# Two-block transformer, float32 as hi and lo halves: four raw weight slots for five, the relative-bias table moved in parts, the first Silu of an FFN earlier

## The reference

```
for l in range(DEPTH):                                   # block 1, DEPTH = 2
    h = h + 0.5 * swiglu(rms_norm(h, ffn1_norm[l]), w1, w3, w2)
    h = h + token_mixer(rms_norm(h, mix_norm[l]), ...)   # attention + pooling branches
    h = h + 0.5 * swiglu(rms_norm(h, ffn2_norm[l]), w1, w3, w2)
h = rms_norm(h, final_norm)
for l in range(DEPTH):                                   # block 2
    x = x + 0.5 * rmsnorm(swiglu_2(rmsnorm(x, ffn1_pre_g[l]), ...), ffn1_post_g[l])
    ...   # y = sum of 3 gated branches (SSD scan, retention, windowed attention) @ w_out
    x = x + rmsnorm(y, mix_post_g[l])
    x = x + 0.5 * rmsnorm(swiglu_2(rmsnorm(x, ffn2_pre_g[l]), ...), ffn2_post_g[l])

swiglu(u) = (silu(u @ w1) * (u @ w3)) @ w2               # d_ff = 2816
```

## Time and profile before

| | us |
|---|---|
| median of 3 runs (lowest to highest) | 2753.46 (2751.01 to 2755.84) |
| the profiled execution | 2757.64 |
| its span, first to last instruction | 2755.9 |
| TensorE busy in it | 2631.7 (95%) |
| VectorE busy | 1544.3 (56%) |
| ScalarE busy | 1222.1 (44%) |
| DMA queue of the weights, share of 16 engines | 50.1% |
| mean granted clock of TensorE | 0.97 of full |

### The profile page before, as it was taken

The page is one execution under the profiler, slowest core; times in us unless marked ns, Lnnn a source line. Parts: engine busy times, 40 slices in busy tenths (PEclk is TensorE's granted clock), DMA queues, the critical chain, the costliest instruction groups (busy, mean ns, idle before and its releaser), DMA issues.

```text
span 2755.9 us, 30036 instructions
## 1 busy us (share of the span) xinstructions
PE 2631.7 (95%) x12238; PEld 2189.7 (79%) x12238; DVE 1544.3 (56%) x1787; ACT 1222.1 (44%) x1530; POOL 54.1 (2%) x71
## 2 busy tenths in 40 slices
PE   7799999999998999999998998999999998998999
PEld 6688778888887887788877877888888877877887
DVE  5345655454565545545556476545555556485554
ACT  5335444444453444445444353544545444453543
POOL 0000000000000000000000000000000000000000
PEclk9899999999999999999999997999999999998999
DMA  6765355555643555655543341555655542442553
GB/s 226 181 223 169 119 163 192 184 184 184 222 160 113 183 184 183 217 185 192 185 163 103 126 151 61 177 191 176 198 192 199 175 161 91 139 138 75 184 192 122
DMA packets 309753, 459.02 MB, mean 167 GB/s; under 512 B 18112, under 2 KB 207856, under 8 KB 309360
## 3 DMA queue, kind: packets, MB, share of 16 engines
q1 hardware_dynamic: 306976, 452.83, 50.1%
q10 hardware_dynamic: 2640, 4.26, 1.1%
HBM read 452.84 MB, written 4.19 MB: 166 GB/s over the span
## 4 chain that ended last, share of the span: by engine, by line
PE 87%; DVE 5%; ACT 3%; issue 2%; DMA 2%; SPq 0%; DVEq 0%; POOL 0%; ACTq 0%
PE acc L588 46%; PE work L588 32%; PE work L595 2%; PE acc L797 2%; PE work L781 1%; ACT w_hi L1024 1%; DVE w_lo L1337 1%; DMA raw<-ffn_w_dram 1%; DMA raw<-w_ffn_in_dram 1%; PE work L993 1%; DVE field L1528 0%; ACT xt_hi L1070 0%; PE work L623 0%; PE work L810 0%; ACT field L1178 0%
## 5 line engine op out<-in xcount | busy, mean ns | idle before, releaser
L1337 DVE TENSOR_TENSOR w_lo<-raw,w_hi 128x2048 fp32r<-128x2048 f32 (+1 forms) x420 | 953.4, 2272 | 784.9 <-ACT w_hi L1024 784.4
L1024 ACT CAST w_hi<-raw 128x2048 fp32r<-128x2048 f32 (+1 forms) x420 | 795.3, 1895 | 606.5 <-PE acc L588 279.4
L588 PE MATMUL work<-w_hi,xt_hi 128*128 128x512 f32 x1408 | 559.7, 397 | 12.3 <-DVE w_lo L1337 5.4
L588 PE MATMUL work<-w_hi,xt_lo 128*128 128x512 f32 x1408 | 550.4, 391 | 0.0
L588 PE MATMUL work<-w_lo,xt_hi 128*128 128x512 f32 x1408 | 549.7, 390 | 0.0
L588 PE MATMUL acc<-w_hi,yt_hi 128*128 128x512 f32 x1088 | 434.7, 400 | 22.9 <-DVE yt_lo L1348 19.5
L588 PE MATMUL acc<-w_hi,yt_lo 128*128 128x512 f32 x1088 | 430.0, 395 | 0.0
L588 PE MATMUL acc<-w_lo,yt_hi 128*128 128x512 f32 x1088 | 429.9, 395 | 0.0
L588 PE MATMUL acc<-w_hi,xt_hi 128*128 128x512 f32 (+2 forms) x896 | 345.2, 385 | 5.9 <-DVE field L1528 4.3
L588 PE MATMUL acc<-w_lo,xt_hi 128*128 128x512 f32 (+2 forms) x896 | 341.8, 381 | 0.0
L588 PE MATMUL acc<-w_hi,xt_lo 128*128 128x512 f32 (+2 forms) x896 | 341.7, 381 | 0.0
(11 more groups left out here) (162 smaller groups left out, 1732.7 us busy)
## 6 DMA issues: line engine op xcount, KB each, us to landing
raw<-ffn_w_dram SPq DMA_DIRECT2D x264, 512.0 KB, 4.5
raw<-w_in_dram SPq DMA_DIRECT2D x204, 512.0 KB, 4.5
raw<-w_ffn_in_dram SPq DMA_DIRECT2D x176, 512.0 KB, 4.8
raw<-w_ffn_out_dram SPq DMA_DIRECT2D x88, 512.0 KB, 4.3
raw<-w_branch_dram SPq DMA_DIRECT2D x48, 512.0 KB, 4.5
raw<-w_out_dram SPq DMA_DIRECT2D x32, 512.0 KB, 4.4
bias<-b_gate_dram SPq DMA_DIRECT2D x10, 512.0 KB, 7.0
raw<-w_branch_attn_dram SPq DMA_DIRECT2D x8, 512.0 KB, 3.9
```

What stands on the lines that cost most here:

```text
L588: last = nc.tensor.matmul(out, x[:, kt, k], y, start=start and n == 0, stop=stop and n == 2)
L1024: nc.scalar.copy(w_hi[:, slot, 0:n], raw[:, at, 0:n]).then_inc(hi_split[slot], 1)
L1337: nc.vector.tensor_tensor(w_lo[:, at, 0:n], raw[:, at, 0:n], w_hi[:, slot, 0:n].bitcast(F32), ALU.subtract).then_inc(unit_split[slot], 1)
```

## The change

It has four parts. (1) `RAWS` goes from 5 to 4: the load of unit p now waits for unit p-4. (2) ACT stores the table in 8 parts of 384 KB, one each in steps 2 to 8 of the first FFN and the eighth after them, and SP loads it in 4 parts of 512 KB in steps 2 to 5 of the first FFN of block 2; `decay` and `rope2` go from step 0 to step 1. (3) In the entry of an FFN the Silu of row 0 and its `hidden` stand ahead of the square of row 1 and of the cast of unit 3, and those of row 1 ahead of the cast of unit 4. (4) At the passage from block 1 to block 2 the transposes of h come behind the last part of the down product.

```diff
-RAWS = 5
+RAWS = 4
+PIECES = 8
...
-            def second_block():
-
-                sp.wait_ge(h_ready, h_count(number[0, depth - 1, "f2"]))
-                for dst, src in ((decay, a["decay"]), (rope2, a["rope2"])):
-                    sp.dma_start(dst, src).then_inc(blk_loaded, 16)
-                sp.wait_ge(scratch_stored, 16)
-
-                sp.dma_start(rel_bias, bass.AP(a["scratch"].tensor, P - 1,
-                                               [[3 * P - 1, P], [3 * P * P, 16], [1, 2 * P]])) \
-                    .then_inc(blk_loaded, 16)
+            def second_block(j):
+
+                if j == 1:
+                    for dst, src in ((decay, a["decay"]), (rope2, a["rope2"])):
+                        sp.dma_start(dst, src).then_inc(blk_loaded, 16)
+                    sp.wait_ge(scratch_stored, 16 * PIECES)
+                if 2 <= j < 6:
+                    g = j - 2
+                    sp.dma_start(rel_bias[:, 4 * g:4 * g + 4, :],
+                                 bass.AP(a["scratch"].tensor, P - 1 + 4 * g * 3 * P * P,
+                                         [[3 * P - 1, P], [3 * P * P, 4], [1, 2 * P]])) \
+                        .then_inc(blk_loaded, 16)
...
-                early = not block and name == "f1"
-                if early:
+                at = 3 if stage + 1 == len(stages) else 2 if stages[stage + 1][0] > block else block or name == "f2"
+                if at == 0:
                     turn_h(stage + 1, 0)
                 down_part(u + 3 * steps - 1, 1, 0, 2, end=True).then_inc(half_summed, 1)
-                if not early and stage + 1 < len(stages):
+                if at == 1:
                     turn_h(stage + 1, 0)
                 down_part(u + 3 * steps - 1, 1, 1, 2, end=True).then_inc(unit_used[slot], 1)
+                if at == 2:
+                    turn_h(stage + 1, 0)
...
                 turn_hi_rows(stage, 1, range(4))
+                if name != "m":
+                    act.wait_ge(rs_ready, norm_count(block, l, "pre_" + name, 0))
+                    silu(u, 0, 0)
                 square_row(1, 4)
                 split(u + 3)
...
-                for r in range(2):
-                    act.wait_ge(rs_ready, norm_count(block, l, "pre_" + name, r))
-                    silu(0, r)
-                    split(u + 4 + r)
+                act.wait_ge(rs_ready, norm_count(block, l, "pre_" + name, 1))
+                silu(u, 0, 1)
+                split(u + 4)
+                split(u + 5)
...
                         act.wait_ge(table_ready, 2)
-                        act.dma_start(a["scratch"], field[0:16, 5000:5384].unsqueeze(1).broadcast_to([16, P, 3 * P])) \
-                            .then_inc(scratch_stored, 16)
+                    if j >= 2 and stage == 0:
+                        store_table(j - 2)
...
+                def store_table(i):
+
+                    n = P // PIECES
+                    act.dma_start(a["scratch"][:, i * n:(i + 1) * n, :],
+                                  field[0:16, 5000:5384].unsqueeze(1).broadcast_to([16, n, 3 * P])) \
+                        .then_inc(scratch_stored, 16)
...
                 turn_lo_rows(stage, 1, range(4))
+                if name != "m":
+                    dve.wait_ge(rs_ready, norm_count(block, l, "pre_" + name, 0))
+                    hidden(ffn_count(block, l, name, 2 * steps), 0, 0)
                 split(u + 3)
```

More of the change, by code:

```diff
@@ L419, in mixer_small, with ffn @@
                         .then_inc(bias_loaded[i], 16)
-            def ffn(block, name, l, between=lambda: None):
+            def ffn(block, name, l, between=lambda j: None):
                 u = first_unit[block, l, name]
@@ L430, in ffn @@
                         small(block, l, name)
-                        between()
+                    between(j)
                 if name == "f1":
@@ L500, in mixer2, with constants @@
                 chunks("w_out_2", 0, 2)
-            def constants():
+            def constants(j):
+                if j:
+                    return
                 sp.dma_start(field[0:32, 4096:4112], a["rel_bias_2"]).then_inc(consts_loaded, 16)
@@ L510, in constants @@
                     .then_inc(post_loaded, 16)
-            def second_block():
-                sp.wait_ge(h_ready, h_count(number[0, depth - 1, "f2"]))
-                for dst, src in ((decay, a["decay"]), (rope2, a["rope2"])):
-                    sp.dma_start(dst, src).then_inc(blk_loaded, 16)
-                sp.wait_ge(scratch_stored, 16)
-                sp.dma_start(rel_bias, bass.AP(a["scratch"].tensor, P - 1,
-                                               [[3 * P - 1, P], [3 * P * P, 16], [1, 2 * P]])) \
-                    .then_inc(blk_loaded, 16)
+            def second_block(j):
[9 more added lines that the diff above has]
+                        .then_inc(blk_loaded, 16)
             for block in range(2):
                 for l in range(depth):
-                    ffn(block, "f1", l, (second_block if block else constants) if l == 0 else lambda: None)
+                    ffn(block, "f1", l, (second_block if block else constants) if l == 0 else lambda j: None)
                     (mixer2 if block else mixer1)(l)
@@ L1072, in turn_hi_rows, with silu @@
                     last.then_inc(xt_hi_ready, 1)
+            def silu(u, j, r):
+                slot, n = used_count(u + 3 * j if j else u + 1, r)
+                act.wait_ge(unit_used[slot], n)
+                nc.scalar.activation(act_gate[:, r, :], work[2 + r][:, 0:NARROW], ACT.Silu,
+                                     scale=rs[:, r:r + 1]).then_inc(silu_ready, 1)
             def enter(stage, end=None):
@@ L1143, in ffn @@
                         act.wait_ge(table_ready, 2)
-                        act.dma_start(a["scratch"], field[0:16, 5000:5384].unsqueeze(1).broadcast_to([16, P, 3 * P])) \
-                            .then_inc(scratch_stored, 16)
+                    if j >= 2 and stage == 0:
+                        store_table(j - 2)
                     split(u + 6 + 3 * j)
                     for r in range(2):
-                        silu(j + 1, r)
+                        silu(u, j + 1, r)
                     split(u + 7 + 3 * j)
@@ L1151, in ffn @@
                 hidden_halves(steps - 2)
+                if stage == 0:
+                    for i in range(steps - 4, PIECES):
+                        store_table(i)
                 split(n - 1)
-                silu(steps - 1, 0)
+                silu(u, steps - 1, 0)
                 split(n)
-                silu(steps - 1, 1)
+                silu(u, steps - 1, 1)
                 hidden_row(0)
@@ L1205, in mixer1 @@
                 ahead(1)
-                act.wait_ge(scratch_stored, 16)
+                act.wait_ge(scratch_stored, 16 * PIECES)
                 act.wait_ge(rs_ready, norm_count(0, l, "pre_m", 1))
@@ L1414, in norm_final, with hidden @@
                                                    ALU.mult).then_inc(h_ready, 1)
+            def hidden(silus_before, j, r):
+                dve.wait_ge(silu_ready, silus_before + (j * 2 + (r + 1)))
+                nc.vector.scalar_tensor_tensor(hid[:, r, :], work[2 + r][:, NARROW:2 * NARROW], rs[:, r:r + 1],
+                                               act_gate[:, r, :], ALU.mult, ALU.mult).then_inc(hidden_ready, 1)
             def enter(stage, end=None, by=0.5):
@@ L1457, in ffn @@
                 silus_before = ffn_count(block, l, name, 2 * steps)
[L1459 to L1463, removed]
                 def hidden_halves(step):
@@ L1476, in hidden_row @@
                                             yt_hi[:, 2:4, k].bitcast(F32), ALU.subtract).then_inc(hidden_split, 1)
[L1478 to L1481, removed]
+                dve.wait_ge(rs_ready, norm_count(block, l, "pre_" + name, 1))
+                hidden(silus_before, 0, 1)
+                split(u + 4)
+                split(u + 5)
                 for j in range(steps - 2):
@@ L1491, in ffn @@
                     for r in range(2):
-                        hidden(j + 1, r)
+                        hidden(silus_before, j + 1, r)
                     split(u + 7 + 3 * j)
@@ L1496, in ffn @@
                 split(n - 1)
-                hidden(steps - 1, 0)
+                hidden(silus_before, steps - 1, 0)
                 split(n)
-                hidden(steps - 1, 1)
+                hidden(silus_before, steps - 1, 1)
                 hidden_row(0)
@@ L1659, in mixer2 @@
                 ahead(5)
-                dve.wait_ge(blk_loaded, 48 * depth + 48)
+                dve.wait_ge(blk_loaded, 48 * depth + 96)
                 pair, n = chunk_count(1, l, "rqk", 1)
```

## The result

| | before | after |
|---|---|---|
| median of 6 runs, us (lowest to highest) | 2754.19 (2745.23 to 2756.05) | 2959.74 (2953.56 to 2963.71) |
| ratio, 95% interval | | 1.075 (1.0729 to 1.077) |
| the profiled execution, span | 2755.9 | 2960.9 |
| TensorE busy | 2631.7 (95%) | 2704.3 (91%) |
| mean granted clock of TensorE | 0.97 | 0.943 |

What follows compares the result with a forecast made beforehand. TensorE, busy 95%, bounds the kernel through its waits and clock. 31 + 7 + 106 + 37 - 15 - 3 - 2 - 2 = +159 us on 2757.6, less 4.2, gave 2913 us, range 2840 to 2965.

Steps and rivals of the forecast that it cites:

- A cast is late by a whole load: With four slots, a cast right behind the use of p-4 starts 4.8 to 5.3 us later.
- Tails, 31 us: Seven FFN tails: hidden of row 1 stands behind the late cast of u+33, TensorE waits 4.4 us each.
- Inner steps, 7 us: 72 inner FFN steps: room for a load is 5.6 us; 12 loads exceed it by 0.6 on average, +7 us.
- Mixers, 106 us of waits: Vector work behind late casts: 23.5 us per block 1 mixer, 29.3 per block 2 mixer, two each; +106 us.
- The clock, 37 us: In tails and mixers, 23 new waits of 4 us or more lose 1.6 us each; bounds 0 to 78.
- The store, -15 us: First FFN's table store in eight parts: 18 us of wait and clock go, +3 charged for delayed loads.
- Part 3, -2 us: FFN entries: waits for the moved hidden go, -3.4, row scale later, +1.5; order of casts behind costs nothing during units 0-2.
- The load time of a unit: Skill page estimates 4.4 us, the trace 5.26; the trace was used, with 4.4 the time would be near 2880.
- (A): Rival, faster: the lead was spare, late casts are hidden and parts 2 to 4 remain; 2731 us, chance 0.04 with (D).
- (D): Rival: loads are limited by something else than the fifth slot, so part 1 gives 0; chance 0.04 with (A).
- (B): Rival, half: mixer delays overlap, 53 for 106, and few waits reach the clock, 15 for 37; 2838 us, chance 0.12.
- (C): Rival: inner steps lose 0.5 us each, 36 for 7, and store parts meet critical loads, 18; 2960 us, chance 0.08.

Runs made afterwards that it cites:

- experiment 6: Changed kernel with Silu and hidden of row 1 and the halves of row 0 ahead of the cast of u+33 in tails; 2935.46 us, 1.0659 of before.
- e1: Changed kernel with RAWS back at 5, so parts 2, 3 and 4 alone; 2722.94 us, 0.9882 of before.
- experiment 5: Changed kernel with five raw slots, but loads of mixer units wait for p-4 and those of FFN units for p-5; 2887.05 us, 1.0489 of before.
- experiment 2: Kernel before with RAWS at 4, part 1 alone; 3009.65 us, 1.0914 of before.
- experiments 7 and 10: Each on the changed kernel: first hidden tile's halves ahead of the cast of u+5, 2940.77 us; block 2's small FFN vectors loaded one step later, 2945.62 us.
- e8: Changed kernel with 18 needless transposes of the identity ahead of the transposes of hidden row 1 in seven tails; 2949.9 us, 1.0712 of before.
- experiment 4: Kernel before with part 3 alone, first Silu and hidden ahead of the square and the cast; 2744.07 us, 0.9961 of before.

## Why the prediction was right, and where it was short

- **A cast is late by a whole load.** Right: 5.38 us in the tail shown (4.8 to 5.3 forecast, and 5.26 measured ahead), and ScalarE's waits went over to the DMAs, by far more than the 300 us I named. The 56.0 of the earlier trace rows was only the largest of the DMA groups; together they were 130 us before and are 1363 after, all of the idle time ahead of casts.
- **Tails, 31 us.** Measured 28.4 us of waits in seven. In five the mechanism is the forecast one, shown by experiment 6; in two it is the load of u+32 behind the mixer's tables, which I had not seen, and that these two have the forecast size is luck.
- **Inner steps, 7 us.** The steps kept their 16.8 us in seven of the eight FFNs but for 1.1 us here or there. In the first FFN they lost 6.2 us, beside the parts of the store. In the other seven the steps are 3.2 us longer in all. The size is right, the spread over all FFNs is not.
- **Mixers, 106 us of waits.** TensorE's idle time there grew by 22.6 + 21.6 (47 forecast) and 30.7 + 27.3 (59 forecast), 102 us. Following each list with the casts put 5 us later works.
- **The clock, 37 us: the term that was mis-sized.** The busy time of TensorE grew by 72.6 us after - before and by 82.5 after - e1. This is most of the 47 us that were missing. The step that failed is the price, not the count. I took 23 new waits of 4 us or more, 1.6 us each. Counted in the traces, the stretches at 0.50 in which TensorE works went from 19 to 45: 26 more. The busy time grew by 2.8 us for each of them, since they are longer than the 3.4 us that I took: in all 164 us before and 331 after, 6.4 more per added stretch. The sum is close to the prediction's own upper bound of 78, which came from the row of 6.8 us. The price is no property of the place either: unit 13 of the first two mixers lost 5.4 and 5.8 us of clock in the changed kernel and some 2.4 in experiment 5, with nearly the same waits; unit 40 of the others lost 4.0 and 3.7.
- **The count itself** came out near for a reason that I didn't have. Behind the start, the changed kernel has 19 waits of 4 us or more, not 23; shorter ones made up for it. Of its 24 waits of 1.8 to 3.0 us that begin at full clock, 18 have a stretch at 0.50 that begins beside them or at most 2.1 us behind; of those of 3.0 and more, all 28. The trace of before had it already: the stretch of 838.7 to 842.1 stands behind this wait of 2.17 us,

```profile
837.84 0.50 PE L588 MATMUL acc<-w_hi,xt_hi 128*128 128x512 f32 x1 [2.17 <-DVE field L1528]
```

  and in a mixer of the changed kernel a wait of 2.29 does the same (columns of the last two rows as in the earlier trace rows):

```profile
853.73 1.42 PE L600 MATMUL work<-ident,field 128*128 128x128 f32 x8 [2.29 <-ACT field L1198]
...
853.40:856.80 3.40, 3.07 (x13) 2.62 (x14) 0.00 (x0) 3.40 (x7) 0.00 (x0) 0.66 0.00 0
856.80:860.20 3.40, 3.40 (x14) 2.72 (x13) 2.26 (x1) 1.10 (x1) 0.00 (x0) 0.84 0.00 0
```

- **The store, -15 us.** -18.0 with five slots and no cost of the parts. With four, -13.4 at the place and +6.2 at four later units, -7; against part 1 alone, whose one large store costs more with four slots, it is -17.7 and +6.2.
- **Part 3, -2 us, and what stands behind it.** This step failed twice. I charged the order only with the waits of before, though part 1 makes the old order cost 45 us (experiment 2): an edit that is worth little by itself pays for another. And I wrote that the casts behind the moved Silu cost nothing while TensorE is on units 0 to 2. The halves of the first hidden tile stand behind the cast of u+5, whose load is slow beside small vectors, and that cost 20 us (experiments 7 and 10).
- **The load time of a unit.** By the Trainium skill, page "SBUF — State Buffer", section "The DMA setup-cost knee", it is an estimate of 4.4 us. In this case's traces a unit took 5.4 us to its cast, and up to 8.4 beside small vectors, so the page's figure was too small here. The total near 2880 that I worked out with it would have been 80 us too low.
- **Rivals.** (A) and (D) are excluded by experiments 1 and 5. (B) is excluded by the mixers' idle time, which grew by 102 us and not by 53. Of (C) only the number came out, 2960: its mechanism, longer inner steps and parts of the store on critical loads, gave 6 us in one FFN.
- **The total.** The 47 us are the difference of two errors: by experiment 1, part 1 costs 237 us for 181 forecast (31 + 7 + 106 + 37), and parts 2 to 4 gain 33 for 22. The waits of part 1, 153 us for 144, are near in sum although the 14.5 us of waits at the first down units were not in it.

## What to carry to other kernels

A buffer that looks spare by count can be the one that lets a load run ahead of the event that frees the next buffer; look at which of two waits ends last ahead of the consumer, and if it is never the load's, ask where the load starts when one buffer is gone. The price isn't paid by the data but by the other work that stands behind the late step in the same engine's list, so follow each list with that step moved. And price each new wait of a TensorE that runs at full clock with about half again on top (82.5 us of clock on 153.4 of waits in this kernel), the waits of 2 us too.

## What the hardware showed that I had not expected

- TensorE's clock fell to half at 18 of the 24 waits of 1.8 to 3.0 us in the changed kernel, and not behind the one of 0.83 in e8. Forty needless transposes of a 128 by 128 tile, 4.53 us, kept the clock at 1.00 where a wait of 4.38 us had lost it; 18 of them, 2.13 us, with a wait of 2.50 behind, did not.
- A small vector read for all 128 partitions stands 1.4 us ahead of a 1 MB load that takes 8.4 us to its cast; with the small vectors moved away the same load takes 5.6.
- With the clock, small shifts matter: experiment 4 gained 7 to 14 us while TensorE's idle time fell by 1.2. Which places give that stays open.
